# First attention of a two-block transformer kernel: one step at a time against two

## The reference

```
q, k, v, z = split(h @ w_in)          # 8 heads; q and k are two halves of 64 per head
o1 = softmax(q1 @ k1.T / 8) @ v       # tokens see 512 keys, context rows see 256
o2 = softmax(q2 @ k2.T / 8) @ v
o  = rms_norm(o1 - lam * o2, subln_g) * (1 - lam_init)
y  = (o * silu(z)) @ w_out
```

## Time and profile before

| | |
|---|---|
| median of 3 runs | 784.1 us (784.07 to 784.76) |
| the profiled execution | 784.2 us |
| its span, first to last instruction | 782.2 us |
| TensorE busy (PE) | 772.2 us, 99% |
| TensorE weight loads (PEld) | 615.6 us, 79% |
| VectorE busy (DVE) | 550.9 us, 70% |
| ScalarE busy (ACT) | 395.6 us, 51% |
| the chain that ended last | PE 84%, DVE 9%, ACT 3% |
| the attention's steps | about 180 to 285 us from the span's start |

### The profile page before, as it was taken

One profiled execution on the slowest core, in us unless ns is written; L12 is line 12 of the kernel. 1 busy time (PEld: TensorE's weight loads), 2 busy tenths in 40 slices (PEclk: granted clock), 3 DMA queues, 4 the chain that ended last, 5 costly groups with the idle time before them and its releaser, 6 DMA issues.

```text
span 782.2 us, 10963 instructions
## 1 busy us (share of the span) xinstructions
PE 772.2 (99%) x4001; PEld 615.6 (79%) x4001; DVE 550.9 (70%) x988; ACT 395.6 (51%) x752; POOL 41.9 (5%) x54
## 2 busy tenths in 40 slices
PE   8999999999999999999999999999999999999998
PEld 5668777887777888867788888787788888888886
DVE  3356999797768868599767666998977545565553
ACT  4462323328788765565656656725454443443431
POOL 0020000000001010112100002200010000000000
PEclk9999999999999999999999999999999999999999
DMA  9995563344000075239122045963225755565621
GB/s 326 356 368 189 215 214 124 108 146 162 2 1 1 1 281 209 100 120 351 66 94 101 5 155 169 377 223 108 84 65 203 259 172 162 194 212 186 200 69 54
DMA packets 75576, 125.76 MB, mean 161 GB/s; under 512 B 2842, under 2 KB 36972, under 8 KB 75396
## 3 DMA queue, kind: packets, MB, share of 16 engines
q1 hardware_dynamic: 74576, 123.00, 45.9%
q10 hardware_dynamic: 532, 1.21, 0.4%
q0 software_dynamic: 416, 0.85, 0.4%
HBM read 123.99 MB, written 1.06 MB: 160 GB/s over the span
## 4 chain that ended last, share of the span: by engine, by line
PE 84%; DVE 9%; ACT 3%; issue 2%; DMA 1%; POOL 1%; SPq 0%; DVEq 0%; ACTq 0%
PE psum L869 16%; PE psum L871 15%; PE psum L870 15%; PE psum L858 4%; PE psum L859 4%; PE psum L860 4%; PE psum L1052 3%; PE psum L1077 3%; PE psum L977 3%; PE psum L1375 3%; PE psum L1373 3%; PE psum L1374 3%; DVE w_lo L1994 2%; PE psum L1150 2%; PE psum L891 2%
## 5 line engine op out<-in xcount | busy, mean ns | idle before, releaser
L870 PE MATMUL psum<-w_lo,act_hi 128*128 128x512 f32 (+1 forms) x624 | 241.9, 388 | 0.0
L869 PE MATMUL psum<-w_hi,act_hi 128*128 128x512 f32 (+1 forms) x584 | 237.4, 406 | 2.6 <-DVE act_lo L2175 1.9
L871 PE MATMUL psum<-w_hi,act_lo 128*128 128x512 f32 (+1 forms) x584 | 226.9, 389 | 0.0
L1994 DVE TENSOR_TENSOR w_lo<-raw,w_hi 128x2048 fp32r<-128x2048 f32 (+1 forms) x68 | 153.2, 2260 | 63.1 <-ACT w_hi L1412 63.0
L1412 ACT ACTIVATE w_hi<-raw 128x2048 fp32r<-128x2048 f32 (+1 forms) x72 | 136.2, 1895 | 70.3 <-PE psum L871 31.1
L869 PEld LDWEIGHTS psum<-w_hi,act_hi 128*128 128x128 f32 x584 | 109.6, 188 | 38.9 <-issue 14.5
L870 PEld LDWEIGHTS psum<-w_lo,act_hi 128*128 128x128 f32 x624 | 117.5, 188 | 20.5 <-issue 0.5
L871 PEld LDWEIGHTS psum<-w_hi,act_lo 128*128 128x128 f32 x584 | 109.6, 188 | 23.4
L1963 POOL TENSOR_TENSOR rstd<-ms,half_neg 128x1 f32<-128x1 f32 (+3 forms) x38 | 36.0, 949 | 523.4 <-DVE ms L2035 523.4
L858 PE MATMUL psum<-act_hi,w_hi 128*128 128x512 f32 x128 | 51.0, 399 | 0.0
L859 PE MATMUL psum<-act_lo,w_hi 128*128 128x512 f32 x128 | 50.0, 391 | 0.0
(11 more groups left out here) (292 smaller groups left out, 1133.4 us busy)
## 6 DMA issues: line engine op xcount, KB each, us to landing
raw<-in_a_w_in SPq DMA_DIRECT2D x16, 1024.0 KB, 8.7
raw<-in_ada_w SPq DMA_DIRECT2D x14, 1024.0 KB, 5.2
raw<-in_w_out SPq DMA_DIRECT2D x12, 1024.0 KB, 5.3
raw<-in_w_gate SPq DMA_DIRECT2D x22, 512.0 KB, 4.0
raw<-in_w_up SPq DMA_DIRECT2D x22, 512.0 KB, 5.1
raw<-in_w_down SPq DMA_DIRECT2D x11, 1024.0 KB, 5.0
raw<-in_b_w_in SPq DMA_DIRECT2D x10, 1024.0 KB, 7.9
raw<-in_w_in SPq DMA_DIRECT2D x10, 1024.0 KB, 5.8
```

What stands on the lines that cost most here:

```text
L869: pe.matmul(oh, x_hi, hi, start=(k == 0), stop=False)
L870: pe.matmul(o[:, 0:n], x_hi, lo, start=False, stop=False)
L871: mm = pe.matmul(oh, x_lo, hi, start=False, stop=(k == KT - 1))
L1994: ins = dve.tensor_tensor(rest, weights, hi.bitcast(F32), ALU.subtract)
```

## The change

Steps are taken in pairs (p even). On TensorE both steps' scores of the next pair stand side by side, then transposes(p), blocks, transposes(p+1), values(p), blocks, values(p+1). The blocks are two a step (before: 1, 3, 1, 3), and units (7, 0) and (7, 1) are interleaved. ScalarE and VectorE get a matching order. ScalarE rounds three of the four weight halves in two pieces (`split_piece`), with a semaphore of its own for the first piece; the fourth goes behind the loop. The diff, cut (`...`); of the tables the two that decide when a unit is complete and when weights are rounded are shown:

```diff
+QUARTERS = [range(0, 2), range(2, 4), range(4, 6), range(6, 8)]
+BESIDE_ATTENTION0 = {p: (6 + p // 16, (p // 4) % NT, QUARTERS[p % 4]) for p in range(NT * HEADS)}
+BESIDE_ATTENTION0.update({16 + i: (7, (i // 2) % 2, QUARTERS[i % 2 + 2 * (i // 4)]) for i in range(8)})
-SPLITS_BESIDE0 = [4, 14, 18, 30]
-RESTS_BESIDE0 = {5: 0, 7: 1, 15: 0, 17: 1, 19: 0, 27: 1}
+SPLITS_BESIDE0 = {4: 0, 6: 1, 14: 0, 16: 1, 18: 0, 20: 1}
+RESTS_BESIDE0 = {6: 0, 8: 1, 16: 0, 18: 1, 20: 0, 26: 1}
```

TensorE:

```diff
-            for p in range(NT * HEADS):
+            def turn0(p):
                 pe.wait_ge(s_comb, p + 1)
                 turn_probs(("t0", p), sc[:, 4 + p % 2, :], XT if STEPS0[p][0] >= XT else NT)
+            for p in range(0, NT * HEADS, 2):
                 if p + 2 < NT * HEADS:
                     scores0(p + 2)
-                c, t, ks = BESIDE_ATTENTION0[p]
-                gemm_unit("in0", c, t, ks)
+                    scores0(p + 3)
+                turn0(p)
+                gemm_unit("in0", *BESIDE_ATTENTION0[p])
+                turn0(p + 1)
...
                 values0(p)
+                gemm_unit("in0", *BESIDE_ATTENTION0[p + 1])
+                values0(p + 1)
```

ScalarE, where `turned0(p)` is the move of step p:

```diff
+            def split_piece(i):
...
+                hi, weights, _ = split_parts(n)[0]
+                r = slice(i * size // 2, (i + 1) * size // 2)
+                if i == 0:
...
+                    seq.note(act.activation(hi[:, r], weights[:, r], ACTF.Copy).then_inc(s_whipart, 1), s_whipart)
+                    return
+                seq.note(act.activation(hi[:, r], weights[:, r], ACTF.Copy).then_inc(s_whi, 1), s_whi)
...
-            for p in range(NT * HEADS):
-                if 0 < p < NT * HEADS - 1:
-                    exp0(p + 1)
-                if p:
-                    beside0(p - 1)
-                    out0(p - 1)
...
+            for p in range(0, NT * HEADS, 2):
+                if p in (26, 28):
+                    to_feature("turn_o0", [0], parts=((p - 26) // 2,))
+                if p:
+                    out0(p - 1)
+                turned0(p)
+                if p + 2 < NT * HEADS:
+                    exp0(p + 2)
+                turned0(p + 1)
+                out0(p)
+                if p + 2 < NT * HEADS:
+                    exp0(p + 3)
                 if p:
                     beside0(p - 1)
...
                 if p in SPLITS_BESIDE0:
-                    split_through(done_halves[0])
+                    split_piece(SPLITS_BESIDE0[p])
+            split_through(done_halves[0])
             beside0(NT * HEADS - 1)
             out0(NT * HEADS - 1)
```

VectorE:

```diff
-            for p in range(2, NT * HEADS):
-
-                if p % 2:
-                    comb0(p)
-                if p + 1 < NT * HEADS:
-                    max0(p + 1)
-                if p % 2 == 0:
-                    comb0(p)
+            for p in range(2, NT * HEADS, 2):
+                comb0(p)
                 if p in (26, 28):
                     to_feature("turn_o0", [0], parts=((p - 26) // 2,))
+                comb0(p + 1)
+                if p + 2 < NT * HEADS:
+                    max0(p + 2)
+                    max0(p + 3)
                 beside0(p - 1)
                 if p in RESTS_BESIDE0:
-                    split_piece(RESTS_BESIDE0[p])
-                if p in (17, 18):
-                    sub_mean(TILES0[p - 17])
-                if p in (21, 23):
-                    gated(0, FIRST if p == 21 else SECOND)
-                if p in (25, 29):
-                    gated(2, FIRST if p == 25 else SECOND)
+                    part = RESTS_BESIDE0[p]
+                    split_piece(part, 0 if part else 1 + len([q for q in RESTS_BESIDE0 if q < p]) // 2)
+                if p in (16, 18):
+                    sub_mean(TILES0[(p - 16) // 2])
+                if p in (22, 24):
+                    gated(0, FIRST if p == 22 else SECOND)
+                if p in (28, 30):
+                    gated(2, FIRST if p == 28 else SECOND)
```

More of the change, by code:

```diff
@@ L140 @@
 ASIDE = {("out1", 1, 1), ("in2", 1, 1), ("in2", 3, 1), ("out2", 0, 0), ("gu", 0, 0), ("down", 0, 0)}
-BESIDE_ATTENTION0 = {p: (6 + p // 16, (p // 4) % NT, [range(0, 1), range(1, 4), range(4, 5), range(5, 8)][p % 4])
-                     for p in range(NT * HEADS)}
-SPLITS_BESIDE0 = [4, 14, 18, 30]
-RESTS_BESIDE0 = {5: 0, 7: 1, 15: 0, 17: 1, 19: 0, 27: 1}
+QUARTERS = [range(0, 2), range(2, 4), range(4, 6), range(6, 8)]
[3 more added lines that the diff above has]
+RESTS_BESIDE0 = {6: 0, 8: 1, 16: 0, 18: 1, 20: 0, 26: 1}
 ROUND_BESIDE1 = {1: 0, 2: 1, 4: 0, 5: 1, 8: 0, 9: 1}
@@ L209, in banks_plan @@
     for p in range(NT * HEADS):
-        if p % HALF_KT == 0:
+        if BESIDE_ATTENTION0[p][2][0] == 0:
             gemm_unit("in0", *BESIDE_ATTENTION0[p][0:2])
@@ L450, in block_kernel @@
         s_sumused, s_summed, s_sumsplit = sem("summed_half_used"), sem("gate_sum_ready"), sem("gate_sum_split")
+        s_whipart = sem("w_hi_first_part_ready")
         s_gatein = sem("first_gate_chunk_in")
@@ L1414, in split_through @@
                     done_halves[0] += 1
+            def split_piece(i):
+                n = done_halves[0]
+                at, size = load_no[halves[n]], half_size(halves[n])
+                hi, weights, _ = split_parts(n)[0]
+                r = slice(i * size // 2, (i + 1) * size // 2)
+                if i == 0:
+                    act.wait_ge(landed[at % RAW], landed_at[at])
+                    act.wait_ge(*slot_free[n])
+                    seq.note(act.activation(hi[:, r], weights[:, r], ACTF.Copy).then_inc(s_whipart, 1), s_whipart)
+                    return
+                seq.note(act.activation(hi[:, r], weights[:, r], ACTF.Copy).then_inc(s_whi, 1), s_whi)
+                done_halves[0] += 1
             def run_chunk(stage, c, unit, before_norm=False, ahead=4):
@@ L1611, in _, with turned0 @@
             run_chunk("in0", 5, last_in0, before_norm=True)
-            for p in range(NT * HEADS):
-                if 0 < p < NT * HEADS - 1:
-                    exp0(p + 1)
+            def turned0(p):
+                n = XT * P if STEPS0[p][0] >= XT else NT * P
+                move(sc[:, 6 + p % 2, 0:n], ("t0", p), n=n, wait_for=("pv0", p - 2) if p >= 2 else None)
+            for p in range(0, NT * HEADS, 2):
[10 more added lines that the diff above has]
+                    exp0(p + 3)
                 if p:
                     beside0(p - 1)
-                    out0(p - 1)
-                n = XT * P if STEPS0[p][0] >= XT else NT * P
-                move(sc[:, 6 + p % 2, 0:n], ("t0", p), n=n, wait_for=("pv0", p - 2) if p >= 2 else None)
                 if p in SPLITS_BESIDE0:
-                    split_through(done_halves[0])
-                if p in (25, 27):
-                    to_feature("turn_o0", [0], parts=((p - 25) // 2,))
+                    split_piece(SPLITS_BESIDE0[p])
+            split_through(done_halves[0])
             beside0(NT * HEADS - 1)
@@ L2006, in run_chunk, with split_piece @@
                     split_through(g0 + ahead)
-            def split_piece(i):
+            def split_piece(i, part_rounded=0):
                 n = done_halves[0]
@@ L2017, in split_piece @@
                     hi, weights, rest = parts[i]
-                dve.wait_ge(s_whi, n + 1)
+                if part_rounded:
+                    dve.wait_ge(s_whipart, part_rounded)
+                else:
+                    dve.wait_ge(s_whi, n + 1)
                 ins = dve.tensor_tensor(rest, weights, hi.bitcast(F32), ALU.subtract)
@@ L2359, in _ @@
             max0(2)
+            max0(3)
             split_through(half_no[("in0", 6, 1)])
-            for p in range(2, NT * HEADS):
-                if p % 2:
-                    comb0(p)
-                if p + 1 < NT * HEADS:
-                    max0(p + 1)
-                if p % 2 == 0:
-                    comb0(p)
+            for p in range(2, NT * HEADS, 2):
+                comb0(p)
                 if p in (26, 28):
                     to_feature("turn_o0", [0], parts=((p - 26) // 2,))
+                comb0(p + 1)
+                if p + 2 < NT * HEADS:
+                    max0(p + 2)
+                    max0(p + 3)
                 beside0(p - 1)
                 if p in RESTS_BESIDE0:
-                    split_piece(RESTS_BESIDE0[p])
-                if p in (17, 18):
-                    sub_mean(TILES0[p - 17])
-                if p in (21, 23):
-                    gated(0, FIRST if p == 21 else SECOND)
-                if p in (25, 29):
-                    gated(2, FIRST if p == 25 else SECOND)
+                    part = RESTS_BESIDE0[p]
[6 more added lines that the diff above has]
+                    gated(2, FIRST if p == 28 else SECOND)
             split_through(done_halves[0])
```

## The result

The changed kernel takes 803.4 us (median of 4 runs, 801.4 to 803.8), the kernel before 784.2: a ratio of 1.0239, 95% interval 1.0227 to 1.0251. It is slower, as forecast, but by 19.2 us and not by 13: outside the range of 788 to 802. The profiled execution took 803.8 us with a span of 801.6. TensorE's busy time in the stretch holds more than its work now, since a part of it runs at half the clock. The granted clock, over the whole of each of the four executions, was 0.989, 0.989, 0.994 and 0.991 (803.8, 803.8, 801.4 and 803.1 us): the same program does not spend the same time at the lower level each time. What follows is read from the first of them.

A forecast was written before the change was run, and what follows sets the result against it. TensorE, 99% busy, was taken to bound the kernel. Terms -5.8 + 17.8 - 0.35 + 1.3 = +12.95 on the profiled 784.2 us gave 797 us; the 8-in-10 range was 788 to 802.

The forecast's parts named there:

- Joining the scores: On TensorE, 30 score blocks become 15, each saving 0.39 us for changes of array height: -5.8 us, up to 7.3 saved.
- The waits on the chain out, exp, tanh, product, comb: In the loop, TensorE waits for a 4.1 us ScalarE and VectorE chain with only 3.0 us of cover: +17.8 us.
- 2.35 ahead of transpose(26): In pair 24, four gated products on VectorE ahead of comb make TensorE wait 2.35 us.
- 0.8 at values(27): In pair 26, act_hi first on ScalarE delays out(26), for which values(27) wait 0.8 us.
- Behind the loop: After the last rounding moves behind move(31) and out(30), tile 1's transposes wait for gated(1): +1.3 us.
- The step that failed is the clock: Rival: behind the wait ahead of transpose(30) the clock falls from 2.4 to 1.2 GHz, +4.8, 802 us; chance 0.10.
- the others are 2.4 at most: Argument against the clock falling: only the wait ahead of transpose(30) is long, TensorE's other waits 2.4 us at most.
- 0.35: At step 30, the late start of values(30) behind move(30) goes, with more products standing between: -0.35 us.
- the unknown sizes named: Transpose behind scores -1.5 to 0, releases and pipelining -2.7 to +2.7, starts after waits up to +1; likeliest 791 to 802.
- same number, nothing between them: Gate products on TensorE taken 2/2/2/2 a step instead of 1/3/1/3: no time effect expected.
- The cover holds: Rival: VectorE and ScalarE run ahead far enough to hide all waits, leaving only -5.8: 778.4 us; chance 0.08.
- a transpose that pays as a gate product does: On TensorE, a transpose behind scores costs the same extra as a gate product there, so the saving stays 5.8 us.

The follow-up runs named there:

- the run with 30 blocks: On the kernel with the tanh first, TensorE's scores of step p+3 stand behind the transposes of step p, giving 30 score blocks again: 786.1 us.
- the run with TensorE kept busy: On the changed kernel, idle 128-column products on TensorE ahead of the transposes that wait for a comb or gated products: 798.0 us.
- the tanh first: On the changed kernel, ScalarE's tanh of a finished gate unit moved to the start of its pair, ahead of out(p-1): 780.0 us, ratio to before 0.9953.
- a single wait of 3.8 us in a kernel without others of that length: On the kernel with the tanh first, the tanh in pair 28 alone put back behind exp(31): 785.9 us.
- the one with a wait of 1.7 us: The tanh first, plus ScalarE's last rounding back behind step 30's move and VectorE's act_lo behind both maxima in pairs 26 and 28: 779.6 us.
- the kernel with blocks one and three: On the kernel with the tanh first, the gate's blocks set to one and three a step again, in the new order: 784.1 us.

## Why the prediction was right about the waits and wrong about the clock

- *Joining the scores*: forecast -5.8, the range to -7.3. The pair went from 6.62 to 6.15, so 15 x 0.47 = -7.0. Of it 0.40 is the change of height by the median of the run with 30 blocks, 0.44 by its steady pair; the remaining 0.03 to 0.07 was not looked for. These 1.2 us more than forecast hid a part of the miss elsewhere: that the result lies only 1.4 us outside the range is partly luck.
- *The waits on the chain out, exp, tanh, product, comb*: forecast 17.8 us. By starts in the trace less the pace of the instruction ahead: 1.10, 2.24, 1.09, 2.29 and 2.38 ahead of the transposes of steps 6, 10, 14, 18 and 24 (forecast 1.1, 2.25, 1.1, 2.4, 2.35), and 3.96 ahead of those of step 30 with 0.69 at values(29) (forecast 4.1 and 0.7). Values that met a late out: 0.95 in the three places that are not in a low stretch (forecast 0.65). Sum 17.5. One place was wrong: I had 2.35 ahead of transpose(26) and 0.8 at values(27), but the first transposes of tile 0 stand between, need the gated products of pair 24 and took 2.8 of it. That moved a wait, it did not change the sum by more than 0.4.
- *Behind the loop*: forecast 1.3, measured 1.2 (starts 1.44 apart for 0.23).
- **The step that failed is the clock**, which the likeliest sum put at nothing. It was a rival with 0.10, tied to the one wait of 4 us and priced at +4.8; "the others are 2.4 at most" stood there as the reason against more. The clock fell four times: at the waits ahead of transposes 10 (2.24) and 18 (2.29), the transposes of tile 0 (2.8) and transpose 30 (3.96). At the first three the lower level began 0.4, 1.1 and 1.4 us after TensorE had started again, at the last 1.3 us before. Excess over the normal pace in the low stretches: 1.6, 1.6, 1.6 and 2.6, together 7.4 us. Behind 2.38 us (transpose 24) it did not fall, nor behind any 1.1. So the runs show 7.4 us in four places, at least 5.4 of them a loss by the run with TensorE kept busy, where the sum had none. The rival was right in kind, too large for its one place (4.8 for 2.6) and blind to the other three.
- *Sum as measured*: -7.0 + 17.5 + 1.2 + 7.4 - 0.35 = +18.8; the spans differ by 19.4. 0.4 of the rest is a later start of step 2's scores (179.99 against transposes at 179.60), 0.2 stay open. This is the account of the profiled execution; the one that took 801.4 us, with a granted clock of 0.994, lost less to the clock.
- *The arithmetic of the range*: the unknown sizes named, -4.2 to +3.7 around 797, give 793 to 801, and not "791 to 802". And behind the loop 1.6 less 0.5 is 1.1, where 1.3 was taken. Neither changes the forecast's failure.
- *The even blocks*, which I called "same number, nothing between them": true of the work. But they are what covers move(p) once the transposes of step p+1 stand ahead of values(p): 4.0 us without them.
- *The cover holds*, the faster rival, fell: in this order followers with 20% to spare did not help, because each chain begins with values(p). With the tanh first they did keep up.
- The Trainium skill (TensorE: Matmul & The Clock Gate, What's actually happening) has TensorE's clock at the lower level when the engine has been idle. The trace agrees: 0.53 granted in 215.95 to 219.40, behind 2.2 idle us. But 2.3 idle us ahead of transpose(24) were followed by none, so how much idleness it takes is left open here.
- On the weight loads the Trainium skill (TensorE: Matmul & The Clock Gate, Step-by-step: what each phase is for) was read as speaking for a transpose that pays as a gate product does. With the tanh first a transpose pays less and the product behind it pays too: the first transpose behind scores takes 0.17 for 0.11, and the first gate product behind the transposes 0.31 for 0.23. What the weight loads have to do with it no run here shows.

## What to carry to other kernels

When two iterations are joined on the bounding engine, ask of every instruction on the other engines what now stands ahead of it: work whose input has long been there (a tanh) must not queue behind work that waits for the bounding engine (out, exp), if anything with a deadline queues behind it in turn (comb). Add up such a chain from start-to-start distances and compare it with the bounding engine's time to the deadline; that sum came out within 0.15 us here at six places; at a seventh it named the wrong instruction as the one that waits. Then give every wait of TensorE of about 2 us a second price, the clock's (here 1.6 to 2.6 us where the clock fell, and it did not fall each time), and note what an "equal" rearrangement was covering.

## What the runs showed of the hardware

- In none of the traces did the granted clock fall behind a wait of 1.1 us; behind waits of 2.24, 2.29, 2.8 and 3.96 it did, behind 2.38 it did not. It did behind a single wait of 3.8 us in a kernel without others of that length. The price was 1.6 us a fall, 2.6 behind the 4 us wait.
- The length of a wait does not settle it: the changed kernel's four executions had granted clocks of 0.989 to 0.994, and the one with a wait of 1.7 us 1.00 in two and 0.998 in three. One of the 12 executions of the kernel with blocks one and three had 0.997 (786.8 us), though its profiled execution has no wait over 0.6 us in the stretch; why is open.
- Products of an identity with itself, issued in the waits, kept the clock at 1.00 in all four executions and were worth 5.4 us, though their results are not used.
- At the lower level products of 512 columns start 0.43 us apart, at the upper one 0.23.
- Scores of 64 rows between operations of 128 rows cost 0.39 us a block with a gate product behind them and 0.40 to 0.44 where a transpose stands behind every other block.
